# Seven block products for eight in the gate and up projections of a two-layer encoder, with SiLU on ScalarE and the transposes moved

## What is computed

```
a, b = split(rms_norm(x, norm_ffn) @ w_gate_up, 2)     # 256 x 5632 each
x = x + (silu(a) * b) @ w_down
```

## Time and profile before

| | |
|---|---|
| median of 3 runs | 2713.4 us (2713.36 to 2713.74) |
| profiled execution | 2713.74 us |
| its span, first to last instruction | 2711.9 us |
| TensorE, VectorE, ScalarE busy | 100%, 74%, 48% of the span |

### The profile page before, as it was taken

One profiled execution on the slowest core, in us unless ns is written; L12 is line 12 of the kernel. 1 busy time (PEld: TensorE's weight loads), 2 busy tenths in 40 slices (PEclk: granted clock), 3 DMA queues, 4 the chain that ended last, 5 costly groups with the idle time before them and its releaser, 6 DMA issues.

```text
span 2711.9 us, 30191 instructions
## 1 busy us (share of the span) xinstructions
PE 2704.2 (100%) x12042; PEld 2241.7 (83%) x12042; DVE 2014.3 (74%) x2639; ACT 1297.3 (48%) x1551; POOL 119.7 (4%) x90
## 2 busy tenths in 40 slices
PE   9999999999999999999999999999999999999999
PEld 7888888888888888888888888888888888888887
DVE  7888566688768676876878885666887687768765
ACT  6555444444444444444454554444444444444443
POOL 0001000122000000000000010001210000000000
PEclk9999999999999999999999999999999999999999
DMA  9554555555555555565555545555555555555553
GB/s 365 196 191 159 183 207 196 199 193 209 188 197 196 201 189 199 193 225 200 188 186 186 192 158 183 202 203 199 187 198 183 203 197 201 189 188 198 199 203 141
DMA packets 77805, 533.78 MB, mean 197 GB/s; under 512 B 8896, under 2 KB 9152, under 8 KB 15072
## 3 DMA queue, kind: packets, MB, share of 16 engines
q1 hardware_dynamic: 74800, 523.67, 53.7%
q0 software_dynamic: 2288, 7.47, 1.0%
q10 hardware_dynamic: 576, 0.71, 0.1%
HBM read 529.72 MB, written 2.10 MB: 196 GB/s over the span
## 4 chain that ended last, share of the span: by engine, by line
PE 97%; DVE 1%; ACT 0%; DVEq 0%; DMA 0%; POOL 0%; issue 0%; SPq 0%
PE acc L384 31%; PE acc L386 31%; PE acc L385 31%; PE acc L424 1%; PE acc L425 1%; PE acc L423 1%; PE acc L488 1%; DVE w_lo L980 0%; PE tr L500 0%; PE tr L424 0%; PE tr L423 0%; PE tr L425 0%; DMA raw<-weights 0%; PE tr L517 0%; PE tr L516 0%; PE tr L518 0%
## 5 line engine op out<-in xcount | busy, mean ns | idle before, releaser
L980 DVE TENSOR_TENSOR w_lo<-raw,w_hi 128x1024 fp32r<-128x1024 f32 x937 | 1151.6, 1234 | 618.5 <-ACT w_hi L654 596.8
L654 ACT ACTIVATE w_hi<-raw 128x1024 fp32r<-128x1024 f32 x943 | 996.7, 1061 | 1238.8 <-PE acc L386 1228.0
L384 PE MATMUL acc<-w_hi,b_hi 128*128 128x512 f32 x1888 | 735.6, 390 | 2.2 <-DVE b_lo L1033 1.4
L385 PE MATMUL acc<-w_lo,b_hi 128*128 128x512 f32 x1888 | 734.6, 389 | 0.0
L386 PE MATMUL acc<-w_hi,b_lo 128*128 128x512 f32 x1888 | 734.6, 389 | 0.0
L384 PE MATMUL acc<-w_hi,a_hi 128*128 128x512 f32 x1880 | 732.5, 390 | 0.0
L385 PE MATMUL acc<-w_lo,a_hi 128*128 128x512 f32 x1880 | 731.6, 389 | 0.0
L386 PE MATMUL acc<-w_hi,a_lo 128*128 128x512 f32 x1880 | 731.5, 389 | 0.0
L384 PEld LDWEIGHTS acc<-w_hi,b_hi 128*128 128x128 f32 x1888 | 354.5, 188 | 76.2 <-DVE b_lo L1033 1.8
L386 PEld LDWEIGHTS acc<-w_hi,b_lo 128*128 128x128 f32 x1888 | 354.5, 188 | 73.8
L385 PEld LDWEIGHTS acc<-w_lo,b_hi 128*128 128x128 f32 x1888 | 354.5, 188 | 73.1
(11 more groups left out here) (205 smaller groups left out, 1217.5 us busy)
## 6 DMA issues: line engine op xcount, KB each, us to landing
raw<-weights SPq DMA_DIRECT2D x484, 1024.0 KB, 4.8
bias<-bias_in POOLq DMA_DIRECT2D x24, 256.0 KB, 4.6
raw<-weights SPq DMA_DIRECT2D x7, 512.0 KB, 9.4
y<-memT_in SPq DMA_DIRECT2D x14, 256.0 KB, 7.0
rows<-mem_in SPq DMA_DIRECT2D x1, 2048.0 KB, 15.8
x<-xT_in SPq DMA_DIRECT2D x1, 2048.0 KB, 20.0
x<-x_in SPq DMA_DIRECT2D x1, 2048.0 KB, 7.4
out<-x SPq DMA_DIRECT2D x3, 512.0 KB, 7.5
```

The lines of the kernel that those rows point to most:

```text
L384: pe.matmul(o, hi[:, kt + k, tok], wh, start=first and k == 0, stop=False)
L385: pe.matmul(o, hi[:, kt + k, tok], wl, start=False, stop=False)
L654: act.activation(w_hi[:, h % SPLIT_SLOTS, :], raw_half(r), ACT.Copy).then_inc(hi_ready, 1)
L980: dve.tensor_tensor(w_lo[:, slot, :], src, w_hi[:, slot, :].bitcast(F32), ALU.subtract).then_inc(lo_ready, 1)
```

## The change

In the gate and up projection of each layer, the chunk pairs with odd j (1, 3, 5, 7, 9) are computed by `pair`, which takes the seven products for one of their four K groups. The pairs with even j stay as they were ("plain pairs"); j = 0 has its own start as before. The parts of the down projection are now fed as j = 1 to 4, 5 to 8, and 9 and 10, with the same number of down chunks as before.

For an odd j VectorE first adds the accumulators to the sums of the products (`gate_pair` for a, `take_b` for b). ScalarE now writes SiLU of a in place of its sigmoid, from PSUM for even j (`silu_acc`) and from SBUF for odd j (`silu_sums`), so that VectorE's multiplication by a falls away. No turn stands in an odd pair any more: the plain pair j has the turn of j-2 and that of j-1. The activation sums for the gate and up products are made once a layer, and loaded again before each part. The memory tokens of the next layer are loaded ten units later.

```diff
-    for j0, n in PARTS:
-        for j in range(j0, j0 + n):
-            if j > 0:
-                order.append(b[j])
-            if j + 1 < ACT_GROUPS:
-                order.append(a[j + 1])
+    for (j0, n), pairs in zip(PARTS, PAIRS):
+        for j in pairs:
+            if j % 2:
+                order += [(w_gu[g * COLS:(g + 1) * COLS], c * ACT_GROUPS + j) for c, g in PAIR_ORDER]
+            else:
+                order += [a[j], b[j]]
         if n == PART:
             for c0 in range(0, NC, 2):
                 order += [(w_down[(j0 + g) * COLS:(j0 + g + 1) * COLS], c0 + c) for c, g in PAIR_ORDER]
...
-MEM_UNIT = N_UNITS - 2 * NC * PART + RAW_SLOTS
-FFN_ORDER = [("a", 0)]
-for p_, (j0_, n_) in enumerate(PARTS):
-    for j_ in range(j0_, j0_ + n_):
-        FFN_ORDER += [("b", j_)] + ([("a", j_ + 1)] if j_ + 1 < ACT_GROUPS else [])
-    FFN_ORDER += [(p_, c_) for c_ in range(NC)]
+MEM_UNIT = N_UNITS - NC * LAST - 6
+FFN_ORDER = [("a", 0), ("b", 0)]
+for p_, pairs_ in enumerate(PAIRS):
+    FFN_ORDER += [(side, j_) for j_ in pairs_ for side in ("a", "b")] + [(p_, c_) for c_ in range(NC)]
...
+            def pair(left, right, hi, lo):
+                group(left, hi, lo, 1, first=True)
+                group(left, hi, lo, 2)
+                group(right, hi, lo, 1, first=True)
+                seven_products(left, right, 3 - left - right, hi, lo)
+                group(left, hi, lo, 3, last=True)
+                group(right, hi, lo, 2)
+                group(right, hi, lo, 3, last=True)
...
                 for p, (j0, groups) in enumerate(PARTS):
-                    for j in range(j0, j0 + groups):
-                        if j > 0:
+                    n.add("s")
+                    for j in PAIRS[p]:
+                        if j % 2:
+                            pair(FFN_ACC["a", j], FFN_ACC["b", j], *A)
+                        else:
+                            chunk(FFN_ACC["a", j], *A)
                             chunk(FFN_ACC["b", j], *A)
-                        n.add("tr")
-                        if j + 1 < ACT_GROUPS:
-                            chunk(FFN_ACC["a", j + 1], *A)
+                            n.add("tr", 2)
                     acc_of = [FFN_ACC[p, c] for c in range(NC)]
                     if groups == PART:
-                        pe.wait_ge(tr_free, n.at("tr"))
+                        n.add("s")
+                        pe.wait_ge(tr_free, n.at("tr", 1))
                         for c in range(0, NC, 2):
-                            left, right = acc_of[c], acc_of[c + 1]
-                            group(left, *B, 1, first=True)
-                            group(left, *B, 2)
-                            group(right, *B, 1, first=True)
...
-                def sigmoid_inner(j, ahead=4, behind=4):
-                    split(ahead)
+                def silu(j, src):
+                    for t in range(TB):
+                        last = act.activation(rows[:, R_U, t, :], src[:, t, :], ACT.Silu, scale=rs_ffn[:, t:t + 1])
+                    return last
+
+                def silu_acc(j):
                     chunk_done(4)
-                    for t in range(TB):
-                        last = act.activation(rows[:, R_U, t, :], acc[FFN_ACC["a", j]][:, t, :], ACT.Sigmoid,
-                                              scale=rs_ffn[:, t:t + 1])
-                    last.then_inc(sig_ready, 1)
-                    split(behind)
-                split(8)
+                    silu(j, acc[FFN_ACC["a", j]]).then_inc(taken[FFN_ACC["a", j]], 1)
+                    act.drain().then_inc(sig_ready, 1)
+
+                def silu_sums(j):
+                    n.add("a_summed")
+                    act.wait_ge(a_summed, n.at("a_summed"))
+                    silu(j, rows[:, R_U, :, :]).then_inc(sig_ready, 1)
+                split(6)
+                load_sums(h_sums, 1)
+                split(2)
                 act.wait_ge(rs_ready, n.at("layer", 2, 2))
+                silu_acc(0)
...
+                    for j in PAIRS[p]:
+                        if j % 2:
+                            split(4 if j == 1 else 6)
+                            split_seven()
+                            split(6)
...
+                            split(1)
+                            silu_sums(j - 1)
+                            split(7)
+                            if j - 2 == j0 and groups == PART:
+                                copy_first()
+                            op_plain(m_hi[:, kts((j - 2) % PART), :])
+                            split(4)
+                            op_plain(m_hi[:, kts((j - 1) % PART), :])
+                            silu_acc(j)
+                            split(4)
...
+                        load_sums(m_sums, p + 2)
+                        for c in range(0, NC, 2):
+                            split(6)
+                            split_seven()
+                            split(6)
+                            n.add(f"acc{3 - FFN_ACC[p, c] - FFN_ACC[p, c + 1]}")
+                        load_sums(h_sums, 1)
                     else:
+                        split(FULL)
...
-                def gate_inner(j, ahead=5, behind=3):
-                    split(ahead)
-                    wait_sig()
-                    take_inner(FFN_ACC["a", j], R_U)
-                    split(behind)
+                def take_b(j):
+                    acc_b, r = FFN_ACC["b", j], inner_rows(j)
+                    chunk_done()
+                    if j % 2:
+                        dve.tensor_tensor(rows_of(r), acc[acc_b][:, :, :], lower_sums, ALU.add
+                                          ).then_inc(taken[acc_b], 1)
+                        n.add(f"acc{acc_b}")
+                        dve.drain()
+                        wait_sig()
+                        for t in range(TB):
+                            dve.scalar_tensor_tensor(out=rows[:, r, t, :], in0=rows[:, r, t, :],
+                                                     scalar=rs_ffn[:, t:t + 1], in1=rows[:, R_U, t, :],
+                                                     op0=ALU.mult, op1=ALU.mult)
+                    else:
+                        wait_sig()
+                        take_inner(acc_b, r)
+
+                def inner_rows(j):
+                    return R_KV if j % 2 else R_MQ
+
+                def turn_inner(j, copied=False):
+                    for part in range(QUADS):
+                        turn(rows_of(inner_rows(j)), part)
+                        split(1)
+                    if copied:
+                        n.add("copied_a")
+                        dve.wait_ge(a_copied, n.at("copied_a"))
+                    op_plain(kts(j % PART))
...
+                def gate_pair(j):
+                    left = FFN_ACC["a", j]
+                    products_out(3 - left - FFN_ACC["b", j])
+                    split(2)
+                    chunk_done()
+                    dve.tensor_tensor(rows_of(R_U), acc[left][:, :, :], upper_sums, ALU.add).then_inc(taken[left], 1)
+                    n.add(f"acc{left}")
+                    dve.drain().then_inc(a_summed, 1)
...
+                    for j in PAIRS[p]:
+                        if j == 1:
+                            split(4)
+                            dve.tensor_tensor(a_raw, h_hi[:, 0:4, :].bitcast(F32), h_lo[:, 0:4, :].bitcast(F32), ALU.add)
                             dve.drain()
+                            operand_sums(h_sums)
+                            split(4)
+                            load_sums_lo(h_sums)
                             split(1)
+                            n.add(f"acc{FFN_ACC['a', 0]}")
+                            take_b(0)
+                        elif j == PAIRS[p][0]:
+                            add_x(p - 1, NC - 1, 4, 0)
                         else:
-                            if j > j0:
-                                gate_inner(j)
-                            else:
-                                add_x(p - 1, NC - 1, 4, 4)
-                            if j == j0 + 1 and groups == PART:
-                                seven_operands()
+                            split(4)
+                            take_b(j - 1)
+                        if j % 2:
+                            seven_first_sums()
+                            gate_pair(j)
+                        else:
+                            turn_inner(j - 2, j - 2 == j0 and groups == PART)
+                            turn_inner(j - 1)
+                            n.add(f"acc{FFN_ACC['a', j]}")
+                            if j - 2 == j0 and groups == PART:
                                 split(2)
-                                seven_operands_lo()
+                                operand_sums(m_sums)
                                 split(2)
                             else:
                                 split(4)
-                        chunk_done()
-                        take_inner(FFN_ACC["b", j], R_MQ)
```

(65 more changed lines are left out.)

48 lines of the change are left out of this document (16 added, 32 removed).

## The result

The changed kernel takes 2728.9 us (median of 4 runs, 2728.49 to 2729.4); the kernel before took 2713.57 us beside it. The ratio is 1.0056, with a 95% interval of 1.0039 to 1.0074: slower by 0.56%, 15.3 us. Forecast were 2726 us, in a range of 2713 to 2740.

A forecast was written before the change was run, and what follows sets the result against it. TensorE was taken to bound the kernel, busy 2704.2 of 2711.9 us and waiting for nobody in the feed-forward part. 2713.74 - 13.6 saved + 26.3 of waits = 2726.4, stated as 2726 us, range 2713 to 2740.

The forecast's parts named there:

- The saving of 13.6 us: Ten pairs each lose one block product of 6 matmuls: 60 x 0.2267 us on TensorE.
- The odd pairs at nothing: Seven-product gate and up pairs cause no stall: TensorE's 42.16 us hide some 32 us of VectorE's work.
- The plain pairs: Even-j pairs: two turns use up the four-slot cushion, halves 9 to 13 come late, 26.3 us in all.
- VectorE's step list: Instants in a plain pair from its first matmul: first transposes 5.2, second turn's 18.95, half 13's low part 33.6 us.
- the term of a plain pair's delay: TensorE's loss by half 13: 2.25 us per plain pair, 3.2 where the turned tile is also copied.
- ScalarE's part: Queued until the last transposes end, then activation part and Silu: half 13's Copy starts only at 32.5 us.
- The lower bound: If ScalarE were not late at all, half 13 comes 1.15 us late: 11 us less, 2715.
- the case of "about half": Rival: ScalarE's part not on the path, or transpose groups a little shorter; 15 us of stalls, 2715, chance 12%.
- The table load at nothing: Silu's table load, one a layer, 1.283 us, hidden behind a0 by the whole cushion; without that cover 2.6 us.
- What would show it: Signs: 60 matmuls fewer, waits at halves 9 to 13 of plain pairs only, summing to 20 to 32 us, Silu 0.67.

The follow-up runs named there:

- the run with the short turn: Changed kernel with three of the four transpose groups of the second turn in each plain pair left out (work left out): 2699.75 us, ratio 0.9947.
- the run with both edits: Changed kernel, same work: VectorE's second turn begins after half 9, stretched to half 14; ScalarE's Silu after half 12, activation part after half 14: 2700.51 us.
- both runs on it: Changed kernel, ScalarE in plain pairs: Silu ahead of the second activation part, 2721.65 us; or two more unused Silu instructions, 2738.82 us.

## Why the prediction was right

- **The saving of 13.6 us** was there: 42.16 us for a pair with seven products in gate and up as in down, and 2699.75 and 2700.51 us in the two runs without stalls, 14.0 and 13.05 us under the kernel before beside them. The two differences lie on both sides of 13.6; the pitch of 0.2267 between starts, and the 1.36 us by which each pair is shorter (43.52 to 42.16), decide. The section "Back-to-back issue gap" of the Trainium skill's page "TensorE: Matmul & The Clock Gate", which the prediction drew on, gives its 216 ns for a matmul by itself and about 131 ns for a stream of weight loads and matmuls. By these figures six matmuls would be an estimated 1.30 or 0.79 us, and the traces agree with neither.
- **The odd pairs at nothing**: right, shown by the run with the short turn and by the 85.68 us between block products in the run with both edits.
- **The plain pairs**: each instant of VectorE's step list was met to 0.15 us. Mis-sized was the term of a plain pair's delay, 2.25 and 3.2 us where 2.52 and 3.42 were measured, so 26.3 in the sum where it was 28.8. The low part of half 13 started 0.14 later than worked out, by half 12 being 0.1 later and a drain of 0.17. Another 0.1 comes from the step behind it: the prediction took a low part for ready 1.14 after its start, which is the distance to VectorE's next instruction, but its record is 1.23 long, and TensorE starts 1.29 after it (853.16 to 854.45), where 1.14 and 0.05 for the semaphore were taken. With the record's length the 0.05 would have fitted.
- **ScalarE's part** is on the path, as said; both runs on it moved as they should. The lower bound made from it was wrong: half 13 "1.15 late" if ScalarE were not late forgets that half 12 is late before it, 1.6 by the prediction's own list and 1.65 as measured. The stalls without ScalarE's part are 21.5 us (28.8 - 7.25), not 15, so that the case of "about half" was priced 6 us too low for that cause. The range didn't depend on it.
- **Silu** takes 687 ns from PSUM and 708 from SBUF, not the 674 of Sigmoid:

```profile
L926 ACT ACTIVATE rows<-acc,stats 128x512 f32<-128x512 f32 x24 | 15.1, 687 | 0.0
L926 ACT ACTIVATE rows<-rows,stats 128x512 f32<-128x512 f32 x20 | 13.2, 708 | 0.0
```

- **The table load at nothing**: right. It is there (1.28 us), ScalarE's next Copy comes late, and the one after that is on time again, since it waits for a slot, 0.57 us. The kernel before with Silu in place of Sigmoid has two such loads as well and took no longer:

```profile
684.00 1.28 ACT L926 ACT_TABLE_LOAD   x1
685.30 1.27 ACT L926 ACTIVATE rows<-acc,stats 128x512 f32<-128x512 f32 x2
686.73 1.06 ACT L663 ACTIVATE w_hi<-raw 128x1024 fp32r<-128x1024 f32 x1 [0.17 <-issue]
```

- **What would show it** was put too simply: "the waits sum to 20 to 32 us" holds for the starts (28.8), not for the view of waits (12.1).

## What to carry to other kernels

When TensorE never waits, an edit that saves it work is judged by the engines that feed it, and not by their busy share, which still fits here (some 40 us of work in 43.5), but by following their queues instruction by instruction against the time at which each operand is wanted: the deadline of the n-th half against the sum of what stands ahead of it. Before giving such a change up, move its work: here the same instructions, with the second turn begun one low part later and spread over five low parts for four, and ScalarE's two pieces moved to match, turned 0.56% slower into 0.49% faster. And don't add up a view of waits where records overlap; take differences of starts.

## What the runs showed that I had not expected

A row of waits of 12.1 us stood for 28.8 us of lost time, and in the run with the turn one half later a row of 4.7 us for about 13. Behind every wait the second matmul comes about 0.1 us late (0.31 to 0.34 for 0.2267), and the view shows nothing of that either; where the next half is late anyway, it is swallowed by the next wait. And two Silus of 512 columns, 1.08 us by their record, have a pitch of 0.95.
